# Gate and up of an FFN as seven block products, down in a second phase

## The reference

```
def rmsnorm(x, g):
    y = x * lax.rsqrt(jnp.mean(x * x, axis=-1, keepdims=True) + RMS_EPS)
    return y * g
def swiglu(x, w_gate, w_up, w_down):
    return (jax.nn.silu(x @ w_gate) * (x @ w_up)) @ w_down

h = h + 0.5 * swiglu(rmsnorm(h, ffn1_norm), ffn1_w_gate, ffn1_w_up, ffn1_w_down)
h = h + token_mixing(rmsnorm(h, mix_norm), ...)   # w_in, gated recurrence of 4 heads, conv of 31 taps, w_out
h = h + 0.5 * swiglu(rmsnorm(h, ffn2_norm), ffn2_w_gate, ffn2_w_up, ffn2_w_down)
return rmsnorm(h, final_norm)[:, N_META:]
```

## Time and profile before

| | |
|---|---|
| median of 3 runs | 2798.98 us (2795.3 to 2802.89) |
| profiled execution | 2799.2 us span, first to last instruction |
| PE busy | 2635.1 us, 94% |
| PEld busy | 2232.0 us, 80% |
| DVE busy | 1331.7 us, 48% |
| ACT busy | 554.6 us, 20% |
| DMA | 119.92 MB, 43 GB/s in the mean |

### The profile page before, as it was taken

How to read it: one execution, slowest core, us unless ns; L and a number is a source line. 1 busy time by engine, 2 the same in 40 slices (tenths; PEclk the granted TensorE clock), 3 DMA queues, 4 the chain that set the end, 5 groups by cost and what they waited for, 6 DMA issues and landing times.

```text
span 2799.2 us, 31878 instructions
## 1 busy us (share of the span) xinstructions
PE 2635.1 (94%) x13699; PEld 2232.0 (80%) x13699; DVE 1331.7 (48%) x1217; ACT 554.6 (20%) x599; POOL 23.1 (1%) x48
## 2 busy tenths in 40 slices
PE   7999999999999999898989779999999999999996
PEld 6888888888888878787878667788888888888884
DVE  4323343233432468877778775533333233333334
ACT  5111111111111132222322333311111111111114
POOL 0000000000000000000000000000000000000000
PEclk9999999999999999999999789999999999999998
DMA  4111111111111121010110201101111111111101
GB/s 130 38 38 39 38 38 35 35 39 38 38 39 31 57 80 46 21 45 26 31 33 33 97 29 57 43 31 38 38 39 38 39 38 38 39 38 31 38 23 75
DMA packets 146064, 119.92 MB, mean 43 GB/s; under 512 B 3841, under 2 KB 127937, under 8 KB 145921
## 3 DMA queue, kind: packets, MB, share of 16 engines
q1 hardware_dynamic: 141312, 98.64, 11.5%
q0 software_dynamic: 4608, 19.04, 1.7%
HBM read 103.18 MB, written 14.48 MB: 42 GB/s over the span
## 4 chain that ended last, share of the span: by engine, by line
PE 81%; DVE 10%; issue 4%; ACT 3%; DVEq 0%; DMA 0%; ACTq 0%; SPq 0%
PE PS L425 75%; DVE H L1214 2%; PE PS L599 2%; DVE T L1207 1%; DVE T L1205 1%; ACT WH L823 1%; DVE COUT L1440 1%; PE PS L604 1%; DVE BF L1329 0%; DVE BB L1329 0%; PE PS L631 0%; DVE AB L1327 0%; DVE WL L1111 0%; PE PS L729 0%; ACT Q L959 0%
## 5 line engine op out<-in xcount | busy, mean ns | idle before, releaser
L425 PE MATMUL PS<-XH,WH 128*128 128x512 f32 (+2 forms) x2976 | 763.0, 365 | 30.3 <-DVE XL L1172 12.1
L425 PE MATMUL PS<-XL,WH 128*128 128x512 f32 (+2 forms) x2976 | 750.2, 360 | 0.0
L425 PE MATMUL PS<-XH,WL 128*128 128x512 f32 (+2 forms) x2976 | 748.0, 360 | 0.0
L425 PEld LDWEIGHTS PS<-XH,WH 128*128 128x128 f32 x2976 | 499.0, 190 | 122.5 <-issue 27.4
L425 PEld LDWEIGHTS PS<-XL,WH 128*128 128x128 f32 x2976 | 500.4, 190 | 88.9
L425 PEld LDWEIGHTS PS<-XH,WL 128*128 128x128 f32 x2976 | 497.8, 190 | 88.1
L1214 DVE SCALAR_TENSOR_TENSOR H<-PS,H 128x1296 f32<-128x1296 f32 (+1 forms) x176 | 263.6, 1498 | 209.3 <-PE PS L425 209.3
L425 PE MATMUL PS<-HH,WH 128*128 128x512 f32 (+2 forms) x1056 | 269.1, 363 | 29.9 <-DVE H L1214 25.2
L1111 DVE TENSOR_TENSOR WL<-WR,WH 128x1024 fp32r<-128x1024 f32 (+1 forms) x171 | 205.6, 1203 | 185.4 <-ACT WH L823 185.3
L823 ACT ACTIVATE WH<-WR 128x1024 fp32r<-128x1024 f32 (+1 forms) x171 | 176.4, 1032 | 488.7 <-PE PS L425 474.7
L425 PE MATMUL PS<-HH,WL 128*128 128x512 f32 (+2 forms) x1056 | 264.6, 359 | 0.0
(11 more groups left out here) (210 smaller groups left out, 1272.4 us busy)
## 6 DMA issues: line engine op xcount, KB each, us to landing
WR<-in_ffn_w_gate SPq DMA_DIRECT2D x44, 512.0 KB, 3.7
WR<-in_ffn_w_up SPq DMA_DIRECT2D x44, 512.0 KB, 3.8
WR<-in_ffn_w_down SPq DMA_DIRECT2D x44, 512.0 KB, 3.5
WR<-in_w_in SPq DMA_DIRECT2D x28, 512.0 KB, 3.9
hsave<-H POOLq DMA_DIRECT2D x8, 648.0 KB, 3.2
XT<-in_x_sample SPq DMA_DIRECT2D x8, 512.0 KB, 10.6
out_sample<-XO SPq DMA_DIRECT2D x8, 512.0 KB, 5.4
H<-hsave POOLq DMA_DIRECT2D x5, 640.0 KB, 4.2
```

What stands on the lines that cost most here:

```text
L425: mm = nc.tensor.matmul(SET[s][:, o:o + b - a], wt[:, wat[0], wat[1]:wat[1] + P], x(a, b), start=first and wt is WH and x is xh, stop=last ...
```

## The change

Gate and up are taken together as a 2x2 block product. The blocks of the weights are A11, A12 (gate, k-tiles 0 to 3 and 4 to 7) and A21, A22 (up); those of the state are B11, B12 (k-tiles 0 to 3, first and second half of the tokens) and B21, B22. Instead of eight block products there are seven (P1 to P7, Strassen's scheme in the form with 15 additions): four sums of weight blocks per chunk (S1 to S4), four sums of token blocks once per FFN, and seven additions on the way out of PSUM. Each product is 4 k-tiles x 3 passes x 2 matmuls of 324 columns (320 in FFN2), and goes to one of three pairs of PSUM banks in turn. The order of the products is P1, P2, P6, P7, P5, P3, P4.

The low parts of four of the token operands are written over H itself; so POOL first copies H to DRAM (`keep`, tensors before0 and before1) and brings it back before the down phase. Weights go through a ring of three half units (AWH, AWL), raw ones in AR and their sums in AS. The hidden chunks are stored by POOL to DRAM (hidden0, hidden1), and after the last chunk a second phase makes down: for each token half, for each two output tiles (`DOWN_UNITS`, 48 units), all 22 hidden chunks are summed in PSUM and H is updated once. Hidden rows come back per token half, into the tiles that the token operands leave free, and are split again by ACT and DVE. The down weights are loaded once for each token half. The loops over chunks are unrolled on all engines.

The final norm is made by token half: squares, sums, root and reciprocal of the first five tiles of tokens stand in the second half's down units, their transposes too (units 30 to 38), and 1/rms is applied in the copy out of PSUM. POOL stores these five, SP the last five.

```diff
+ORDER = ("P1", "P2", "P6", "P7", "P5", "P3", "P4")
...
+F_GROUPS = ((0, 1, 2, 3), (4, 5, 6, 7), (16, 17, 18, 19), (8, 9, 10, 11), (12, 13, 14, 15), (20, 21))
...
+DOWN_UNITS = [(0, (d, d + 1), g) for d in range(0, KD, 2) for g in F_GROUPS]
+DOWN_UNITS += [(1, (d, d + 1), g) for d in range(0, KD - 2, 2) for g in F_GROUPS]
+DOWN_UNITS += [(1, (d,), g) for d in (KD - 2, KD - 1) for g in F_EIGHTS]
+DOWN_STEPS = [(u, h, d, f) for u, (h, ds, fs) in enumerate(DOWN_UNITS) for f in fs for d in ds]
...
+            def ffn(i, w_gate, w_up, w_down):
...
+                    if m >= 2:
+                        sp.wait_ge(low_left, product_at(i, m - 2, "P4") + 1)
...
+                    for buf, w, loaded in ((2 * b, w_gate, gate_loaded), (2 * b + 1, w_up, up_loaded)):
+                        sp.dma_start(by_k(AR[:, buf, :]), cols(w)[:, :, m * P:(m + 1) * P]).then_inc(loaded[b], 16)
...
+                    load(DOWN_SLOTS[u], src, lambda v: v[:, 0:len(fs) * len(ds) * P].rearrange("p (c n) -> p c n", c=len(fs)))
...
+            def keep(i, lo, k, h):
+                hw = (T - lo) // 2
+                a = lo + h * hw
+                pool.dma_start(before[i][k][:, a:a + hw], H[:, k, a:a + hw]).then_inc(kept[k // KH][h], 16)
...
+                for m in range(NF - 1):
+                    store(m)
+                for after, fs in (("P2", F_GROUPS[0]), ("P6", F_GROUPS[1]), ("P5", F_GROUPS[2] + F_GROUPS[3]),
+                                  ("P4", F_GROUPS[4] + F_GROUPS[5][:1])):
+                    pool.wait_ge(product_done, product_at(i, NF - 1, after) + 1)
+                    for f in fs:
+                        hidden_back(i, lo, 0, f)
+                store(NF - 1)
+                hidden_back(i, lo, 0, NF - 1)
+                for k in range(KD):
+                    pool.dma_start(H[:, k, lo:T], before[i][k][:, lo:T]).then_inc(kept_in[k // 2], 16)
+                for f in F_ORDER:
+                    pool.wait_ge(step_done, i * NSTEP + F_END[0, f])
+                    hidden_back(i, lo, 1, f)
+            for b in range(2):
+                pool.wait_ge(t_free[b], 6 - b)
+            for k in range(KD):
+                for h in range(2):
+                    keep(0, 0, k, h)
+            ffn(0, 0)
             for k in range(KD):
                 pool.wait_ge(sq_ready, k + 1)
                 pool.dma_start(hsave[k], H[:, k, :]).then_inc(h_saved, 16)
...
+                    for at_, p in enumerate(ORDER):
+                        n = product_at(i, m, p)
+                        q_ = m * NPROD + at_
+                        pe.wait_ge(low_left, n + 1)
...
+                            for w, x in ((AWH, x_high(p, kk)), (AWH, x_low(p, kk, lo)), (AWL, x_high(p, kk))):
+                                for q in range(2):
+                                    first = kk == 0 and not seen.get(q)
+                                    seen[q] = True
+                                    mm = nc.tensor.matmul(PAIR[q_ % 3][:, q, 0:qw], w[:, slot, kk * P:(kk + 1) * P],
+                                                          x[:, q * qw:(q + 1) * qw], start=first,
+                                                          stop=kk == KH - 1 and w is AWL)
+                        mm.then_inc(product_done, 1)
+                        seen.clear()
+                        if m == 0 and p == "P2":
+                            if i:
+                                row_sums(norm, lo)
+                        if m == 0 and p == "P3":
+                            spread_r(norm, lo)
...
-                gate_up(xnorm)
-                gate_up()
-                with looped(pe, 0, (GROUPS - 1) // 2, ffn_counts(uses, tiles)) as t:
-                    for g in range(2):
-                        gate_up()
-                        down(g, t * 4 + (hid0 + 2 * g + 2))
-                        gate_up()
-                down((GROUPS - 1) % 2, hid0 + NF, leave if hid0 else None, last=True)
+                        for what in FINAL.get(u, ()) if i else ():
+                            if what == "sums":
+                                half_sums(0)
+                            else:
+                                leave(what)
...
+                    if d in (0, 1):
+                        pe.wait_ge(hidden_left, (2 * i + h) * NF + F_ORDER.index(f) + 1)
...
+                    for wt, x in ((WH, tile_r(hid_high(f))), (WH, tile_r(hid_low(f))), (WL, tile_r(hid_high(f)))):
+                        for q in range(2):
...
+                            mm = nc.tensor.matmul(bank[:, q, 0:qw], wt[:, slot, col:col + P], x[:, q * qw:(q + 1) * qw],
+                                                  start=opens, stop=last and wt is WL)
+                    mm.then_inc(step_done, 1)
...
+                def begin():
+                    if i:
+                        act.wait_ge(t_full[1], OUT_T[1] + 4)
+                    for kk in range(KH):
+                        cast("P1", kk, H[:, kk, lo:lo + hw], g(kk))
+                    for kk in range(KH):
+                        nc.scalar.activation(tile_f(T1_LOW[kk])[:, 0:hw], H[:, kk, lo:lo + hw], ACT.Copy,
+                                             scale=g(kk)).then_inc(x_scaled, 1)
+                    if i:
+                        squared(2, KD - 1, META)
+                    for kk in range(KH):
+                        cast("P2", kk, H[:, kk + KH, lo:lo + hw], g(kk + KH))
+                    for kk in range(KH):
+                        act.wait_ge(x_summed, (4 * i + 1) * KH + kk + 1)
+                        cast("P6", kk, tile_f(T2_LOW[kk])[:, 0:hw])
+                    for kk in range(KH):
+                        act.wait_ge(kept[0][1], 16 * KH * (i + 1))
+                        nc.scalar.activation(H[:, kk, lo + hw:T], H[:, kk, lo + hw:T], ACT.Copy,
+                                             scale=g(kk)).then_inc(x_scaled, 1)
...
+                def p1_low():
+                    for kk in range(KH):
+                        dve.wait_ge(kept[0][0], 16 * KH * (i + 1))
+                        if i:
+                            dve.wait_ge(sq_ready, KD + kk + 1)
+                        dve.wait_ge(x_scaled, (2 * i) * KH + kk + 1)
+                        left("P1", kk, HR[:, kk, first], H[:, kk, first], g(kk))
...
+                def token_sums():
+                    for kk in range(KH):
+                        dve.wait_ge(x_scaled, (2 * i) * KH + kk + 1)
+                        summed(0, kk, t1(kk), H[:, kk, second], g(kk), t1(kk))
+                    for kk in range(KH):
+                        group_done(0, kk)
+                        summed(1, kk, t2(kk), H[:, kk + KH, second], g(kk + KH), t1(kk))
+                    for kk in range(KH):
+                        group_done(1, kk)
+                        dve.wait_ge(kept[1][0], 16 * KH * (i + 1))
+                        if i:
+                            dve.wait_ge(sq_ready, KD + KH + kk + 1)
+                        summed(2, kk, H[:, kk + KH, first], H[:, kk + KH, first], g(kk + KH), t2(kk))
...
+                def lo_of(q):
...
+                    dve.wait_ge(high_cast, n + 1)
...
+                    tt(AWL[:, slot, :], src, AWH[:, slot, :].bitcast(F32), ALU.subtract).then_inc(low_left, 1)
...
+                    if p == "P5":
+                        dve.wait_ge(chain_taken, taken_at(i, m, "s167") + 1)
+                        tt(q3, bank, q2, ALU.add).then_inc(chain_taken, 1)
+                        ins = tt(q1, bank, q1, ALU.add)
+                    if p == "P3":
+                        dve.wait_ge(chain_taken, taken_at(i, m, "s165") + 1)
+                        ins = tt(q1, bank, q1, ALU.add)
...
+                def take_down(h, d):
+                    at_ = h * KD + d
+                    dve.wait_ge(step_done, i * NSTEP + TILE_END[h, d])
+                    dve.wait_ge(kept_in[d // 2], 32 * (i + 1))
+                    v = by_bank(H[:, d, lo + h * hw:lo + (h + 1) * hw])
+                    stt(v, PAIR[DOWN_BANKS[at_]][:, :, 0:qw], 0.5, v, ALU.mult, ALU.add).then_inc(down_taken, 1)
...
+                lo_of(0)
+                p1_low()
+                lo_of(1)
+                p2_low()
+                start()
+                token_sums()
+                p6_low()
+                for q, (m, p) in enumerate(made):
+                    at_ = q % NPROD
+                    if q and at_ != 1:
+                        take_product(*made[q - 1])
+                    lo_of(q + 2)
+                    if m and at_ == 0:
+                        scale_gate(m - 1)
+                    if m and at_ == 1:
+                        scale_up(m - 1)
+                    if m and at_ == 2:
+                        make_hidden(m - 1)
+                    if m == 0:
+                        if at_ == 0:
+                            p7_low()
+                        if at_ == 1:
+                            p5_low()
+                        if at_ == 2:
+                            p3_low()
```

(69 more changed lines are left out.)

845 lines of the change are left out of this document (585 added, 260 removed).

## The result

The kernel after takes 2661.35 us (median of 4 runs, 2659.51 to 2662.52), the kernel before beside it 2799.32 (4 runs, 2795.3 to 2802.89). The ratio is 0.9506, with a 95% interval of 0.9493 to 0.9519: faster by 138 us, 29 us less than the forecast. The profiled execution took 2661.98 us, its span is 2660.0.

What follows compares the result with a forecast made beforehand. TensorE, busy 94%, was taken as the bound: columns streamed times pace, plus its stands. FFN1 -76.0, FFN2 -79.1 and tail -12.5 sum to -167.6 us, from 2799.2 (median 2798.98) to 2632; range 2605 to 2695, forecast 60% (2615 to 2665).

Steps and rivals of the forecast that it cites:

- Pace and steady chunks: Gate/up and down products: a pair takes 0.297 us (FFN1) or 0.294 (FFN2); VectorE's feeding of steady chunks costs nothing.
- Rival (a): All products: a fixed cost per matmul makes them 1760.7 us instead of 1716.3, total 2676; chance 10%.
- rival (b): Gate/up chunks: VectorE sets every chunk's pace, 26.9 us against 25.0, losing 84 us, total 2716; chance 8%.
- Rival (d): All matmuls: weight loads set the pace, 490 us more, total 3122, slower than before; chance 4%.
- P1 at 31.5: FFN1's start: P1 waits for H's copy to DRAM to land and starts near 31.5 us against 30.44.
- From P6 to P6: First to second chunk: VectorE has 35.7 us of work where seven products need 25; 10.7 us lost.
- The start loss: First chunk of each FFN: TensorE waits for operands formed on VectorE, 25.2 us lost in FFN1, 29.4 in FFN2.
- Gate/up to down, 2 us per FFN: Start of the down phase: hidden rows return and VectorE finishes behind the last product; 2 us lost per FFN (0 to 30).
- rival (c): Down phase: it starves for hidden rows, 30 us per FFN, total 2690; chance 10%.
- FFN2's transposes among units, 6: FFN2's down units: 40 transposes of the first token half take 5 us, sums 0.6; 6 with waits.
- The tail, 15.4: Behind FFN2's last product: final additions, norm, transposes and store landing take 15.4 us against 28 now, saving 12.5.
- under 11: Sign at the kernel's end: out-stores start under 11 us after the last product.

Runs made afterwards that it cites:

- the eighth product: Kernel after with P4 computed twice in every chunk but the first, the second overwriting the first: 2810.59 us, ratio 1.0024.
- the narrow matmuls: Kernel after with each gate/up product from the second chunk on made as 48 matmuls of half the width: 3192.16 us (one run).
- the three edits: Kernel after with second-half low parts spread over units 20 to 23, 1/rms spread behind P4 and next P1, FFN1's H copies in order of use: 2628.69 us, ratio 0.9392.

## Why the prediction was right in kind, and 29 us short

**Pace and steady chunks: right.** I took 0.297 and 0.294 for a pair; in the steady stretches it is 0.2966 and 0.2933. The means of the chain, 0.2979 and 0.2941, are 2.5 us above the forecast over FFN1 and nothing over FFN2; 1.6 of the 2.5 are the low clock at P4's start, a price of the late start and not of the columns. Rival (a) needed 0.305. The Trainium skill ("TensorE: Matmul & The Clock Gate", Back-to-back issue gap) gives N/2.4 + 2.5 ns, which would be 137.5 ns at 324 columns (an estimate by that page). The run shows 148.3: not in agreement here, by 11 ns. VectorE is busy 344.72 us in the steady 518.20, 16.6 per chunk (I had 17.9), so rival (b) is out; the eighth product confirms it. Rival (d) asked for a load price of 0.162 us or more, the point from which the kernel would be slower than before; the narrow matmuls put the floor at 0.1116, and 324 columns are 37 ns above it.

**P1 at 31.5: 2.1 late.** I had let seven copies of 324 KB pass at the full rate from 22.3 on. POOL starts the first at 23.28 and gives each 0.54 us, so the seventh is issued at 26.56 and lands 6.0 us later, among all sixteen (VectorE waited until 32.58 for it). My sum had neither the time of issuing nor the copies behind. With the needed four in front P1 starts at 30.73. In FFN2 P1 came 7.5 us after the last output product and not 4.8: H's last addition (1.5 us) stands before the token operands, and ACT has two weight casts (1.15) ahead of them; I had left out both.

**"From P6 to P6", 35.7: too low, by its missing queue.** Up to P6 the sum of VectorE times was even 2.1 too high (19.5 us from P1, where I had 21.6). Behind it I costed 1/rms as VectorE time alone. It is issued on TensorE ahead of P4, and P4's weight part, ready at 73.6, waited until 82.86. The start loss was 27.8 against 25.2 in FFN1 and 30.8 against 29.4 in FFN2; the errors before and behind P6 partly cancelled.

**Gate/up to down, 2 us per FFN: the step that failed.** Measured about 10 in each. I looked for the loss only at the start of the phase (rival (c)), and there the waits were 2.5 and 3.0 us, by late weights more than by late rows. The larger part, 7 us in each FFN, is at the change of token halves, a place that the sum did not have: eight low parts (6.0 us) in a unit of 3.6 us, ahead of the take that TensorE waits for. The experiment that spreads them shows this term by itself: 13.4 us for both FFNs in the spans without the mixing, where the two terms here make 14.

**FFN2's transposes among units, 6: right.** Down there takes 326.1 us, where 1056 pairs are 310.5. Of the 15.6 between them the waits at the start (3.0) and the change of halves (7) leave 5.6 for the transposes, which is a remainder and no measurement of its own.

**The tail, 15.4: 1.6 low.** The chain of after behind the last product, in order of time:

```profile
2643.01 0.84 DVE H L1700
...
2645.51 1.29 PE PS L589 x10
...
2647.14 1.94 PE PS L614 x8
```

Eight transposes take 1.94 us here and took 1.03 in the earlier trace rows, where TensorE was busy between them; in the tail it is idle for 2.9 of the 4.2 us before them and runs at the lower level (granted clock 0.50 from 2647.2 to 2653). I had priced them at the warm row. The last store lands 2.6 us after its issue where I had 5.4 of the earlier trace rows, which hid most of that error, by luck: the first store starts 7 us after the last product, but the last one 14, where I had asked for under 11.

In sum FFN1 is 14.9 us over, FFN2 11.7, the tail 1.6: 28.2 of the 29.

## What to carry to other kernels

When a stage is cut by arithmetic, the steady part can be priced from single rows to within 0.3%; the loss sits at the seams. List every seam, also those in the middle of a phase (here the change of token halves), and compare for each the work that one engine has queued there with the length of the unit that is to cover it. Count a step on every engine on which it is issued: a small product that waits in TensorE's queue stops the large ones behind it, and moving it behind the next product that is ready brought P4 9.4 us forward with nothing made shorter. And take a stretch that the change leaves alone out of both times before you explain a few us.

## What the runs showed of the hardware

- At the full clock an fp32r matmul with its own weight load starts every 148.3 ns at 324 columns, 146.6 at 320, and every 111.6 ns at 162 and 160 alike. From 320 columns and the 234 ns of 512 the line is 0.455 ns a column and 1 ns; it meets the floor near 243 columns (an estimate; no run has that width). An LDWEIGHTS has a mean of 188 to 193 ns in the rows of large products at any of these spacings, so its duration is not its price.
- A stand of 4.7 us cost 7.0, since TensorE went on at 1.2 GHz (granted clock 0.50 in the first 4 us after it and 0.82 in the 19 us around it, 1.00 without the stand).
- A 512 KB load of weights landed in 3.5 us in the median of the execution, and beside rows of 324 KB brought in by another queue in 12.0 (after, DMA engines 96% busy between 600 and 640 us) and 11.2 (with the three edits).
- The unchanged mixing took from 801.1 to 814.0 us in nine profiled executions of kernels that are the same there. A difference of a few us is better read from a span without it than from a median.
